# Attention scores of a two-block transformer kernel: full float32 products against three products of rounded parts, split in place head by head

## The reference

```python
s = (jnp.einsum('bqhd,bkhd->bhqk', qn_b, k_nope)
     + jnp.einsum('bqhd,bkd->bhqk', qr_b, k_rope))
p = jax.nn.softmax(s.astype(jnp.float32) * scale, axis=-1)
return jnp.einsum('bhqk,bkhd->bqhd', p.astype(v.dtype), v)
```

## Time and profile before

| | us |
|---|---|
| median of three runs | 3293.64 (3290.55 to 3300.49) |
| the profiled execution, its own time | 3294.87 |
| its span in the trace | 3292.8 |
| PE busy | 3191.4 (97%) |
| DVE busy | 2071.6 (63%) |
| ACT busy | 1259.9 (38%) |
| POOL busy | 824.0 (25%) |

### The profile page before, as it was taken

One profiled execution on the slowest core, in us unless ns is written; L12 is line 12 of the kernel. 1 busy time (PEld: TensorE's weight loads), 2 busy tenths in 40 slices (PEclk: granted clock), 3 DMA queues, 4 the chain that ended last, 5 costly groups with the idle time before them and its releaser, 6 DMA issues.

```text
span 3292.8 us, 61177 instructions
## 1 busy us (share of the span) xinstructions
PE 3191.4 (97%) x26432; PEld 2520.7 (77%) x26432; DVE 2071.6 (63%) x2965; ACT 1259.9 (38%) x2177; POOL 824.0 (25%) x700
## 2 busy tenths in 40 slices
PE   8999999999999988999999999999999999999998
PEld 7678776777777777467888888878677878888887
DVE  5263475566666565846899877762455575565686
ACT  4333333444444433024433344443333343333444
POOL 1232242111111121200477650000000026666100
PEclk9999999999999999999999999999999999999999
DMA  3251244112211220543122346522101422332753
GB/s 150 67 158 45 71 168 159 41 41 63 63 41 45 64 99 17 181 148 119 73 103 99 119 150 239 174 92 91 39 32 49 155 88 84 113 109 96 251 171 115
DMA packets 125005, 344.32 MB, mean 105 GB/s; under 512 B 15600, under 2 KB 16256, under 8 KB 121920
## 3 DMA queue, kind: packets, MB, share of 16 engines
q1 hardware_dynamic: 103584, 255.99, 23.5%
q0 software_dynamic: 21152, 84.42, 6.9%
HBM read 245.46 MB, written 94.90 MB: 103 GB/s over the span
## 4 chain that ended last, share of the span: by engine, by line
PE 84%; DVE 9%; ACT 4%; issue 1%; DMA 1%; POOL 0%; SPq 0%; DVEq 0%; ACTq 0%; POOLq 0%
PE ps L355 43%; PE ps L354 39%; PE ps L358 3%; DVE AR L364 2%; DVE X L364 1%; DVE SM L375 1%; DVE WS L364 1%; ACT HT L1172 1%; ACT W L361 1%; ACT AR L361 1%; DVE HT L368 1%; DVE W L364 1%; ACT W L2108 0%; ACT WS L361 0%; DVE EX L364 0%
## 5 line engine op out<-in xcount | busy, mean ns | idle before, releaser
L364 DVE TENSOR_TENSOR WS<-W,WS 128x512 fp32r<-128x512 f32 (+1 forms) x284 | 338.3, 1192 | 251.7 <-ACT WS L361 251.4
L354 PE MATMUL ps<-HH,WS 128*128 128x512 f32 x1280 | 394.1, 389 | 0.0
L354 PE MATMUL ps<-TO,WS 128*128 128x512 f32 x1440 | 345.9, 389 | 0.0
L361 ACT ACTIVATE WS<-W 128x512 fp32r<-128x512 f32 (+1 forms) x284 | 210.0, 739 | 313.9 <-PE ps L355 170.6
L354 PEld LDWEIGHTS ps<-TO,WS 128*128 128x128 f32 x1440 | 270.3, 188 | 56.1
L354 PEld LDWEIGHTS ps<-HH,WS 128*128 128x128 f32 x1280 | 240.2, 188 | 50.0
L354 PE MATMUL ps<-HL,WS 128*128 128x512 f32 x640 | 249.0, 389 | 0.0
L354 PE MATMUL ps<-TO 128*128 128x512 f32 x936 | 226.8, 390 | 0.2 <-DVE TO L364 0.2
L355 PE MATMUL ps<-AR 64*64 64x64 f32 (+2 forms) x5440 | 202.1, 241 | 18.5 <-ACT AR L361 4.7
L354 PE MATMUL ps<-WS 128*128 128x512 f32 x888 | 215.1, 390 | 0.1
L361 ACT ACTIVATE X<-ps 128x512 f32<-128x512 f32 (+1 forms) x168 | 100.5, 598 | 295.3 <-PE ps L355 126.9
(11 more groups left out here) (352 smaller groups left out, 6256.3 us busy)
## 6 DMA issues: line engine op xcount, KB each, us to landing
AR_b<-h_d SPq DMA_DIRECT2D x154, 256.0 KB, 2.9
AR<-rw_d SPq DMA_DIRECT2D x104, 256.0 KB, 4.0
W<-in_w_fg SPq DMA_DIRECT2D x44, 512.0 KB, 3.8
W<-in_w_fu SPq DMA_DIRECT2D x44, 512.0 KB, 4.7
h_d<-FST POOLq DMA_DIRECT2D x20, 1024.0 KB, 4.4
x_d<-X POOLq DMA_DIRECT2D x24, 512.0 KB, 4.5
W<-in_w_tok SPq DMA_DIRECT2D x24, 512.0 KB, 3.2
rw_d<-X POOLq DMA_DIRECT2D x40, 256.0 KB, 3.4
```

The costliest lines, as they stand in the source:

```text
L354: return pe.e.matmul(o, l, r, start=start, stop=stop, skip_group_check=True)
L361: return e.e.activation(o, x, ACT.Copy)
L364: return e.e.tensor_tensor(o, x, y, op)
```

## The change

Q and K of a head now have one buffer each (`AQT`, `AKT`, in `HT`). Each is split into a rounded part and the rest (`AQH`, `AKH`, `AQL`, `AKL`, in `HH`, which is free in this stretch). ACT makes the two rounded copies and DVE the two differences, in a new step `rounded` ahead of the first score step of every head; that makes 170 steps. PE makes six rounded matmuls a tile where there were two of float32. Since there is only one set of buffers, SP issues the load of head h+1 behind the last scores of head h (`i % 8 == 7`, with a wait on them), and ACT waits for the load and for those scores before it overwrites `AQH` and `AKH`. V keeps its two buffers and gets a semaphore of its own, for which PE waits in `pv`.

```diff
--- before.py
+++ after.py
@@ -1065,8 +1065,8 @@
 
         MAIN, SIDE = BANKS[0:6], BANKS[6:8]
 
-        AQT = [HT[0:96, 2048 * i:2048 * i + 1024] for i in range(2)]
-        AKT = [HT[0:96, 2048 * i + 1024:2048 * i + 2048] for i in range(2)]
+        AQT, AKT = HT[0:96, 2048:3072], HT[0:96, 3072:4096]
+        AQH, AKH, AQL, AKL = [HH[0:96, 1024 * i:1024 * i + 1024] for i in range(4)]
         AVH = [v3(HT[:, 4096 + 512 * i:4608 + 512 * i], 8) for i in range(2)]
         APB = [HT[:, 5120 + 1024 * i:6144 + 1024 * i] for i in range(2)]
         AOT = [OTB, HT[:, 7168:7680]]
@@ -1078,14 +1078,17 @@
 
             return i // 8, i % 8 // 2 + 4 * (i % 2)
 
-        def att_steps(scores, transp, pv, load, later=lambda i: None):
+        def att_steps(scores, transp, pv, load, later=lambda i: None, rounded=lambda h: None):
             load(0)
             yield
             for i in range(66):
-                if i % 8 == 4 and i // 8 + 1 < 8:
-                    load(i // 8 + 1)
                 if i < 64:
+                    if i % 8 == 0:
+                        rounded(i // 8)
+                        yield
                     scores(i)
+                    if i % 8 == 7 and i < 63:
+                        load(i // 8 + 1)
                     yield
                 if 1 <= i <= 64:
                     transp(i - 1)
@@ -1105,21 +1108,26 @@
                 x = h % 2
                 if h == 0:
                     sp.wait_ge(*at("pe_gate", 31))
+                else:
+                    sp.wait_ge(*at("pe_att", "sc", 8 * h - 1))
+                sp.e.dma_start(AQT, a["qk_d"][h, 0]).then_inc(*dma(f"dma_head{x}", h, "q"))
+                sp.e.dma_start(AKT, a["qk_d"][h, 1]).then_inc(*dma(f"dma_head{x}", h, "k"))
                 if h >= 2:
                     sp.wait_ge(*at("pe_att", "pv", 4 * (h - 2) + 3))
-                sp.e.dma_start(AQT[x], a["qk_d"][h, 0]).then_inc(*dma(f"dma_head{x}", h, "q"))
-                sp.e.dma_start(AKT[x], a["qk_d"][h, 1]).then_inc(*dma(f"dma_head{x}", h, "k"))
-                sp.e.dma_start(AVH[x], a["v_d"][h].rearrange("p (t n) -> p t n", t=8)).then_inc(*dma(f"dma_head{x}", h))
+                sp.e.dma_start(AVH[x], a["v_d"][h].rearrange("p (t n) -> p t n", t=8)).then_inc(*dma(f"dma_of{x}", "v", h))
             return att_steps(skip, skip, skip, load)
 
         def att_pe(pe):
             def scores(i):
                 h, q = head_tile(i)
                 b = take(pe, "sc", i, n=2, banks=SIDE)
-                pe.wait_ge(*at(f"dma_head{h % 2}", h))
+                pe.wait_ge(*at("ve_att", "k", h))
+                qs = slice(q * P, (q + 1) * P)
                 for j in range(2):
-                    x = mm(pe, ps[:, b + j, :], AQT[h % 2][:, q * P:(q + 1) * P], AKT[h % 2][:, j * 512:(j + 1) * 512],
-                           True, True)
+                    o, ks = ps[:, b + j, :], slice(j * 512, (j + 1) * 512)
+                    mm(pe, o, AQH[:, qs], AKL[:, ks], True, False)
+                    mm(pe, o, AQL[:, qs], AKH[:, ks], False, False)
+                    x = mm(pe, o, AQH[:, qs], AKH[:, ks], False, True)
                 x.then_inc(*pe.sig("pe_att", "sc", i))
 
             def transp(i):
@@ -1133,6 +1141,7 @@
             def pv(m):
                 h = m // 4
                 b = take(pe, "pv", m, banks=MAIN)
+                pe.wait_ge(*at(f"dma_of{h % 2}", "v", h))
                 pe.wait_ge(*at("ae_att", "pT", 2 * m + 1, 1))
                 for j in range(8):
                     for y, cols_ in enumerate(ROWS):
@@ -1161,7 +1170,13 @@
             def transp(i):
                 if i == 63:
                     scale(i)
-            return att_steps(scores, transp, skip, skip)
+
+            def rounded(h):
+                ve.wait_ge(*at("ae_att", "q", h))
+                tt(ve, AQL, AQT, AQH.bitcast(F32), ALU.subtract).then_inc(*ve.sig("ve_att", "q", h))
+                ve.wait_ge(*at("ae_att", "k", h))
+                tt(ve, AKL, AKT, AKH.bitcast(F32), ALU.subtract).then_inc(*ve.sig("ve_att", "k", h))
+            return att_steps(scores, transp, skip, skip, rounded=rounded)
 
         def att_ae(ae):
             def later(i):
@@ -1191,7 +1206,13 @@
                     ae.wait_ge(*at(f"dma_oa{h % 2}", h - 2, 1))
                 cp(ae, AOT[h % 2][:, q * P:(q + 1) * P], ps[:, bank("pv", m), 0:P]).then_inc(
                     *ae.sig("ae_att", "o", m, frees=("pv", m)))
-            return att_steps(skip, transp, pv, skip, later=later)
+            def rounded(h):
+                ae.wait_ge(*at(f"dma_head{h % 2}", h, "k"))
+                if h:
+                    ae.wait_ge(*at("pe_att", "sc", 8 * h - 1))
+                cp(ae, AQH, AQT).then_inc(*ae.sig("ae_att", "q", h))
+                cp(ae, AKH, AKT).then_inc(*ae.sig("ae_att", "k", h))
+            return att_steps(skip, transp, pv, skip, later=later, rounded=rounded)
 
         def att_ge(ge):
             def pv(m):

```

## The result

| | before | after |
|---|---|---|
| median (range) | 3293.64 (3290.55 to 3300.49), 5 runs | 3306.41 (3301.89 to 3310.15), 5 runs |
| profiled execution, own time / span | 3294.87 / 3292.8 | 3301.89 / 3300.1 |

The ratio is 1.0035, 95% interval 1.0020 to 1.0049: 11.5 us slower (the two medians alone differ by 12.8), where 15 us faster was forecast, and outside the range given.

What follows compares the result with a forecast made beforehand. PE's own work was taken to set the pace. The terms -32.6 + 3.3 + 9.5 + 3.5 + 1.5 = -14.8 us, from 3294.87, gave 3280 us, range 3266 to 3298.

Steps and rivals of the forecast that it cites:

- Score products: PE's scores: six rounded products take 1.40 us where two float32 took 1.91; 64 tiles give back 32.6 us.
- Cover lost: Less score work on PE to cover the recurrences' round trips through ACT and DVE: a tenth of the gain, 3.3 us, lost.
- The steps: The eight added steps, one at each head, have no PE work in them and cost no time of their own.
- The waits at the heads: At heads 1 to 7, PE waits for DVE's second difference before the scores, 0.7 to 2.35 us each: 9.5 us.
- +3.5 behind: After a head's scores, PE finds DVE's late recurrence work unfinished: 0.5 us a head, 3.5 us in all.
- +1.5 at the start: At the first head, rounding has no work to hide behind: 1.5 us, between 0 and 5.
- The load: K's load at a change of head, landing at 8.4 us, at worst 11.3, is hidden by three rounds: no cost.
- GpSimd beside DVE: Rival: GpSimd operations lengthen DVE's differences, up to 11 us in seven heads, 3291; even chance about 2 us; chance 0.06.
- The slower rival: K lands late, PE stands still about 3.6 us and the clock falls at every head: 7.0 us each, 3316; chance 0.09.
- The end: Attention should end near 1145 us, and the recurrences 15 us earlier than before.
- The bounds: Lower and upper limits of the forecast's terms, from which its own spread was given as 3272 to 3289 us.

Runs made afterwards that it cites:

- the products alone: Six rounded products a tile, Q and K split for head 0 only and used by all heads, against the kernel before: 3288.02 against 3294.12 us, ratio 0.9972.
- both pairs of runs: Empty step at each head added to the kernel before: ratio 1.0014; empty step at the other seven heads added to the products alone: 0.9986 against 0.9972.

## Why the prediction was wrong, step by step

- **Score products, -32.6 us: the step that failed most.** The group takes 1.58 us and not 1.40: -21.1. The rate of 0.234 us was right; the two ends of the group were left out. The 1.91 us of the float32 group had been read from start to next start and hold 0.20 us of ends, and the 1.40 us of the new one, reckoned by the rate inside a stream, hold none. Counted alike, the gain is four intervals of 0.429 against six of 0.234, 0.31 us. The first weight load, named in an expectation as the cause, could be the longer first interval at most, not the last. The Trainium skill's figure in TensorE: Matmul & The Clock Gate, section on the back-to-back issue gap, by which six would have taken 1.29 us, was further off.
- **Cover lost, +3.3 us: mis-sized.** With the products alone PE's idle time rose by 7.1 us. The runs make products and cover together -9 (alone) to -13 us (in the changed kernel), where the prediction had -29.3. These two terms are 16 to 20 of the 26 us between forecast and result.
- **The steps, 0 us: wrong.** They cost 0.14%, 5 us, in both pairs of runs; the first is just clear of chance, the second is not by itself, and both profiled stretches are longer. "No PE work in them" was true; that the recurrences' end isn't moved by how attention lies against them was not. By what alignment they cost stays open.
- **The waits at the heads, +9.5, with +3.5 behind and +1.5 at the start: right in sum, wrong in kind.** PE waited 11.6 us for `HH`, 1.78 of it at the first head; 2.90, 1.93, 2.90 at heads 3, 4 and 7, 0.34 to 0.71 at the others, against 1.6, 2.35, 1.6 and 0.7 to 1.25. Rounding and loads cost 16 us in all, against 14.5, so the sum came out by luck. The wait wasn't the price: without it the time stayed, and with the work but no wait it was 26 us. The knock-on of "0.5 us a head" is the main term, and most of it is DVE's.
- **The load, 0 us: right.** Median 4.6 us, never waited for.
- **GpSimd beside DVE**, given 2 us: right. At heads 3 and 7 a difference took 2.28 and 2.29 us against 1.22 by the median, each begun 0.1 us behind a GpSimd product of 1.3 us: 2.1 us in all. The Trainium skill, in SBUF — State Buffer, on its two separate sides, has such a pair exclude each other for a whole instruction; these rows agree.
- **The slower rival** had the sign right for the wrong cause. K was never late. The clock did fall, at two heads, and holding it up gained about 1 us. Its price appeared in full only with 27.2 us of waits. It wasn't what made this change slower.
- **The end** came 6.5 us later instead of 15 earlier; attention's last product came at 1170.5, where 1145 was forecast: its 170 steps go by rounds of the recurrences, and a round that is held up moves all that follow.
- **The bounds.** The upper ends of the terms (8.2, 10.5 and 5 us beside the 9.5) add up to 3295, not to the 3289 that the forecast's own spread was given. The measured time is above both.

In sum: -9 for products and cover, +5 for the steps, +16 for the rounding, 12 us slower. That this meets the measured 11.5 is no test: each of the three is the difference from one kernel to the next on the way from the one before to the changed one, so they must add up. The kernels were not all run on one chip, and each has an interval of plus or minus 3 to 5 us. Shown is what the three parts cost; that most of the third is DVE's rests on the two runs with one engine's work each; why the steps cost, and what alignment does, stays open.

## What to carry to other kernels

Price the old and the new group of instructions alike: both from their start to the next group's start, or both by the rate inside. When work is added to an engine that others wait for, its cost can be the delay of what is queued behind it, even if that engine is idle for a third of the time and nobody waits for the added work: here differences on DVE in lumps of 2.4 us cost 14 us, ACT's copies in lumps of 2 nothing measurable. Try such work spread over steps, and on the engine that the rest needs least, but with enough rounds of lead that the slower engine isn't waited for. Where lists are interleaved by hand, measure also the bare steps, for one more or fewer moved this kernel by 0.1 to 0.5%.

## What the runs showed that was not expected

- The same GpSimd offload was the worst of all kernels (1.0098) with the rounding in one step, and the best of those that do all the work (0.9981) with it spread over four. Of the worst one's 26 us beyond the changed kernel 14 were PE's longer busy time, at a mean clock of 0.96.
- The length of a wait alone did not tell whether the clock fell. In the changed kernel 2.90 us at head 3 was followed by a window at 0.50, and 1.93 at head 4 left the clock at 1.00. With the float32 products back it was the other way round: 2.90 us at head 3 left it at 1.00, and 1.93 at head 4 came with windows at 0.65 and 0.67. Soon after the start of attention the changed kernel has one at 0.66 (from 560), and no wait of PE just ahead of it was longer than 1.06 us; in the one before it PE was busy for 3.18 of 5 us.
- Filling 7 us of PE's waits with idle products held the clock at 1.00 at the changes of head and gained about nothing.
